# Compression products in quarters between the projection's column units, with bias tables, sigmoid and masks moved up

## The chip, the core and the metric

The kernel runs on one core of one Trainium2 chip. A core has TensorE (PE in the profile; its weight loads are PEld), VectorE (DVE), ScalarE (ACT), GpSimd (POOL) and SyncE (SP), and 16 DMA engines. TensorE runs at one of two clock levels, 1.2 or 2.4 GHz; the profile gives the granted clock as a share of the upper one (PEclk 1.00 or 0.50). The metric is the device time of one execution in microseconds (us); less is better.

## The reference, cut to what matters

The program is two transformer blocks in float32 over 512 positions of width 1024. Only the beginning of the first block is touched: the projection of the normalized input by `w_in`, the compression of two of its column groups (`kc`, `vc`), and the entry of the attention that follows.

```python
def nsa_compress(kraw, pos, w1, b1, w2):
    ch = kraw.reshape(b, g, s // CMP_STRIDE, CMP_STRIDE, dh)
    blk = jnp.concatenate([ch[:, :, :-1], ch[:, :, 1:]], axis=3) + pos
    hid = jax.nn.gelu(jnp.einsum('bgnld,ldh->bgnh', blk, w1) + b1)
    return hid @ w2
...
    xn = rms_norm(h, norm1_g[layer])
    aq, ak, av, bq, kc, vc, ksl, vsl, kw, vw, gl = split_columns(xn @ w_in[layer])
    o_a = mixer_dilated(to_heads(aq, A_HEADS), to_heads(ak, A_HEADS), to_heads(av, A_HEADS), tab_a)
    ...
    k_cmp = nsa_compress(to_heads(kc, B_KV_HEADS), cmp_pos[layer], cmp_k_w1[layer], ...)
    v_cmp = nsa_compress(to_heads(vc, B_KV_HEADS), cmp_pos[layer], cmp_v_w1[layer], ...)
```

`gl` passes through a sigmoid and gates three attention branches. Each head's scores get a bias by distance, which lies as a table per head in DRAM (`bias_spread`).

## The kernel before, in words

The program is a list of stages. Each engine goes through the stages in the same order, and at the end of each all four compute engines meet (`meet`: drain, count up, wait for the four; seen as L2712). SP alone runs ahead: it fills a ring of six weight slots of 1 MB (`Ring.fill`, L254), and for load n it waits until n - 5 slots have been given back (`weights_used`). A DMA from POOL or SP is only issued there; it lands later on a semaphore.

The stage in question is `Together(ModStart, BiasSpread, Load, InProjection)`. On POOL, `BiasSpread` writes the bias tables to DRAM (L933) and `Load` fetches small tensors (L752); nothing else is on POOL there. `InProjection` has six blocks of columns (0 to 5); each has two ring slots, and its work is cut into 28 units (0 to 27), each with a PSUM bank of its own out of banks 0 to 3. Blocks 2 to 5 have four units each of 16 recorded passes of 512 columns (L1040, or L1042 where rows of the input are the weights): units 12 to 15, 16 to 19, 20 to 23, 24 to 27. Even units are copied out of PSUM by DVE, odd ones by ACT (L324, L326, L327). At the end of a block PE drains and gives two slots back (L1046).

`Compress` sits whole behind block 3. DVE has built its inputs after block 2 (`blocks`, L986 and L987; tile `Z`). PE then runs 128 matmuls of 31 columns for K and V (L966, 256 recorded passes, four ring slots loaded by SP as `in_cmp_k_w` and `in_cmp_v_w`, each slot in two DMAs of 512 KB), each half followed by a drain (L969); ACT applies the gelu (L1002), and PE makes four small matmuls more (L973, L977), which DVE copies out (L993, L995).

Behind all units ACT takes the sigmoid of the gates (L1067) and DVE negates `sink`, casts `glamask` and multiplies the gates (L1080 to L1084). Then the engines meet, and `PairAttention` begins. Its first instructions on POOL load the bias tables of the first two packs of heads (`Z<-bias_spread`, L729, four DMAs of 256 KB). PE makes scores (L540), DVE adds the bias and takes the row minimum (L668, waits for the table), ACT takes the exponential (L604), PE transposes (L558) and multiplies by the values (L575). One set of score banks is in use, so the scores of the next unit wait for L668 of this one.

Of the kernel before, what the change touches and what calls it, by code (L numbers as in the profile page):

```python
# [21 lines left out]
P = 128  # L22
# [409 lines left out]
class PairAttention(Stage):  # L432
# [203 lines left out]
    def vector(self, dve, ch):  # L636
# [4 lines left out]
        for i in range(N + 4):  # L641
# [73 lines left out]
            self._copies(dve, "dve", i - 1)  # L715

    def gpsimd(self, pool, ch):
        k = self.k
        if self.loads:
            pool.wait_ge(k.bias_spread, 16)  # L720
        todo = list(self.extra.items())
        for q, heads in enumerate(self.loads):
            if q >= 2:

                while todo and self.packs[todo[0][0]]["load"] < q - 2:
                    self._sum(pool, *todo.pop(0))
                pool.wait_ge(k.bias_used.sem, self.b_used + q - 1)
            for h, src in enumerate(heads):
                pool.dma_start(k.bias[:, q % 2, h, :], src).then_inc(k.bias_landed[q % 2].sem, 16)  # L729
        for pi, x in todo:  # L730
            self._sum(pool, pi, x)
# [204 lines left out]
class Compress(Stage):  # L936


    def __init__(self, k, A, kraw, vraw):
        super().__init__(k)  # L940
        self.raw = [kraw, vraw]
        self.slots = []
        for w1 in (A["cmp_k_w1"][0], A["cmp_v_w1"][0]):
            for l0 in (0, 16):
                src = w1[l0:l0 + 16].rearrange("l d h -> d l h")
                parts = [((lambda s, g=g: s[64 * g:64 * g + 64, :].rearrange("p (l h) -> p l h", l=16)), src) for g in range(2)]
                self.slots.append(k.rg.plan(parts))
        self.blk_ready = k.step_done.reserve(2)
        self.hid_full = k.psum_full.reserve(2)
        self.hid_done = k.gates_done.reserve(2)  # L950
        self.kc_full = k.psum_full.reserve(2)
        self.blk = [k.cmpblk(i) for i in range(2)]
        self.hid = k.cmphid

    def tensor(self, pe):
        k = self.k
        for i in range(2):
            pe.wait_ge(k.step_done.sem, self.blk_ready + i + 1)
            for half in range(2):
                n = self.slots[2 * i + half]  # L960
                k.rg.await_landed(pe, n)
                w = k.rg.slot(n).rearrange("p (l h) -> p l h", l=16)
                for l in range(16):
                    for g in range(2):
                        ll = 16 * half + l
                        last = pe.matmul(k.ps[:, 4 + 2 * i + g, 0:NCMP], w[64 * g:64 * g + 64, l, :],  # L966
                                         self.blk[i][64 * g:64 * g + 64, :, ll], start=(ll == 0), stop=(ll == 31))
                k.rg.released(last)
            pe.drain().then_inc(k.psum_full.sem, 1)  # L969
# [26 lines left out]

    def scalar(self, act, ch):
        k = self.k
        for i in range(2):
            act.wait_ge(k.psum_full.sem, self.hid_full + i + 1)  # L1000
            for g in range(2):
                act.activation(self.hid[:, i, g * NCMP:(g + 1) * NCMP], k.ps[:, 4 + 2 * i + g, 0:NCMP],  # L1002
                               ACT.Gelu_apprx_tanh, bias=k.b1[:, i:i + 1])
            act.drain().then_inc(k.gates_done.sem, 1)


class InProjection(Stage):


    READY, INSIDE = 2, 3  # L1010

    def __init__(self, k, w, blocks, load, compress):
        super().__init__(k)
        self.slots, self.units, self.load = [], [], load
        for b, items in enumerate(blocks):
            c0, cn = items[0][1], sum(x[2] for x in items)
            self.slots.append((cn, [plan_columns(k, w, k0, 4, c0, cn) for k0 in (0, 4)]))
            for kind, at, n, dst, scale in items:
                self.units += [(b, kind, at - c0, n, t, dst, scale) for t in (range(ST) if kind == "rows" else [0])]
            if b == self.INSIDE:  # L1020
                self.compress = compress()
        owners = ["act" if dst is None else x for x, (*_, dst, _) in zip(alternate(len(self.units)), self.units)]
        self.banks = Banks(k, owners, 0, 4, lane=1)
        self.gated = k.step_done.reserve(1)

    def last_of(self, b):
        return max(u for u, x in enumerate(self.units) if x[0] == b)

    def tensor(self, pe):
        k = self.k  # L1030
        for u, (b, kind, at, n, t, _, _) in enumerate(self.units):
# [5 lines left out]
            for c in range(DK):  # L1037
# [3 lines left out]
                else:  # L1041
                    last = pe.matmul(self.banks.bank(u)[:, 0:n], k.HT[:, c, t * P:(t + 1) * P], w,  # L1042
                                     start=(c == 0), stop=(c == DK - 1))
            self.banks.filled(last)
            if u == self.last_of(b):
                pe.drain().then_inc(k.weights_used, 2)  # L1046
                if b == self.INSIDE:
                    self.compress.tensor(pe)

# [11 lines left out]
    def scalar(self, act, ch):  # L1061
        k = self.k
        for u, x in enumerate(self.units):
            self._take(act, "act", u)
            if u == self.last_of(self.INSIDE):
                self.compress.scalar(act, ch)
        act.activation(k.gate3[:, :, :], k.Zb(IN_W)[:, :, GL:GL + 24], ACT.Sigmoid).then_inc(k.step_done.sem, 1)  # L1067

    def vector(self, dve, ch):
        k = self.k  # L1070
        for u, x in enumerate(self.units):
            self._take(dve, "dve", u)
            if u == self.last_of(self.READY):
# [3 lines left out]
                self.compress.blocks(dve)  # L1077
            if u == self.last_of(self.INSIDE):
                self.compress.taken(dve)
        dve.tensor_scalar(k.sink[:, :], k.sink[:, :], -1.0, None, ALU.mult)  # L1080
        dve.tensor_copy(k.glamask[:, :, :], k.maskf)
        dve.wait_ge(k.step_done.sem, self.gated + 1)
        g = k.gate3[:, :, :].rearrange("p t (h b) -> p t h b", b=3)[:, :, :, 0]
        dve.tensor_tensor(g, g, k.cmpvalid[:, :].unsqueeze(2).to_broadcast((P, ST, 8)), ALU.mult)  # L1084

# [1239 lines left out]
def two_blocks(nc, A, C, out, scratch):  # L2325
    ctx = ExitStack()
    with ctx:
# [223 lines left out]
        def rows(at, n, mine=False):  # L2551
# [7 lines left out]
        start, spread, small = ModStart(k), BiasSpread(k, bias_rows, scratch["bias"], scratch["spread"]), Load(k, pairs)  # L2559
        add(Together(k, start, spread, small,  # L2560
                     InProjection(k, A["w_in"][0], blocks, small, lambda: Compress(k, A, rawT[:, 0, :], rawT[:, 1, :]))))

# [16 lines left out]
        for rr in range(4):  # L2579
# [9 lines left out]
            loads.append([bias_of(A_HEADS + rr), bias_of(A_HEADS + 4 + rr)])  # L2589
        add(PairAttention(k, packs, 512, 7168, 9216, 1, 4, loads))  # L2590

# [232 lines left out]
```

## Time and profile before

| | before |
|---|---|
| median of 3 runs | 2438.12 us (2437.29 to 2439.75) |
| the profiled execution | 2439.43 us, span 2437.6 us |
| mean granted clock | 0.925 |
| PE busy | 2093.0 us (86%) |
| DVE, ACT, POOL busy | 1001.9, 601.7, 183.2 us |

The page first gives busy time by engine, then the span in 40 slices (61 us each): the busy tenths of each engine, the clock granted to PE, and the share of the DMA engines. PE is busy 86% of the span, more than twice as long as any other engine, so a stretch of the program is read by when PE works, at which clock, and for what it waits. The page's own chain of waits covers only the last microseconds and says nothing on this stage; the timeline and the tables by stretch do.

### The profile page before, as it was taken

How to read it: one execution, taken by the hardware profiler on the slowest of the kernel's cores; microseconds unless marked ns; L12 is line 12 of the kernel's file. 1: busy time of each engine (PE TensorE's matmuls, PEld its weight loads, DVE VectorE, ACT ScalarE, POOL GpSimd, SP SyncE). 2: the span in 40 equal slices, each digit the busy share in tenths (PEclk: the TensorE clock that was granted, in tenths of full speed). 3: DMA queues.
4: the chain of work that ended last, by engine and by line, in shares of the span. 5: the costliest groups of instructions: out<-in, count | busy, mean ns of one | idle time of the engine just before them, and what ended most of it. 6: DMA issues, size and time to landing. Idle time of an engine off the chain costs nothing. (4 is left out here: it accounts for less than half of the span.)

```text
span 2437.6 us, 26968 instructions
## 1 busy us (share of the span) xinstructions
PE 2093.0 (86%) x10260; PEld 1126.0 (46%) x10260; DVE 1001.9 (41%) x1847; ACT 601.7 (25%) x1138; POOL 183.2 (8%) x219
## 2 busy tenths in 40 slices
PE   5998999899999996989988975999629688958993
PEld 3564774444444443565566453333225466443331
DVE  1001660478773003686344135223155655243333
ACT  1002660100000003322254022333231344023441
POOL 3000110011110000121000000000010000001001
PEclk9988999899999998999999976999859899968997
DMA  7532101476664212111010034777531000055994
GB/s 224 114 104 95 36 10 52 157 257 242 232 235 138 78 54 91 35 35 70 4 49 2 17 123 169 261 299 290 185 127 70 1 1 1 1 201 215 348 343 147
DMA packets 103757, 311.66 MB, mean 128 GB/s; under 512 B 8727, under 2 KB 42679, under 8 KB 85200
## 3 DMA queue, kind: packets, MB, share of 16 engines
q1 hardware_dynamic: 73360, 178.50, 21.1%
q0 software_dynamic: 23040, 105.19, 12.4%
q10 hardware_dynamic: 7232, 26.25, 2.8%
q8 instruction: 85, 1.39, 0.2%
q14 instruction: 40, 0.33, 0.0%
HBM read 280.47 MB, written 34.68 MB: 129 GB/s over the span
## 5 line engine op out<-in xcount | busy, mean ns | idle before, releaser
L2294 PE MATMUL ps<-wide 128*128 128x512 f32 x704 | 306.0, 594 | 2.1 <-issue 1.3
L2057 PE MATMUL ps<-wide,Z 128*64 x576 | 258.7, 603 | 3.5 <-DVE Z L2151 3.5
L2058 PE MATMUL ps<-T,Z 128*64 128x512 f32 x576 | 258.7, 602 | 0.0
L2294 PEld LDWEIGHTS ps<-wide 128*128 128x128 f32 x704 | 132.4, 190 | 171.6 <-issue 170.6
L294 PE MATMUL ps<-wide 128*128 128x512 f32 x448 | 196.8, 601 | 5.5 <-ACTq L2712 4.3
L604 ACT ACTIVATE T<-T,nm 128x128 f32<-128x128 f32 (+5 forms) x208 | 139.7, 672 | 176.3 <-DVE nm L668 176.3
L376 PE MATMUL ps<-ident,T 128*128 128x128 f32 x240 | 39.5, 345 | 143.5 <-DVE T L365 143.5
L558 PE MATMUL ps<-ident,T 128*128 128x128 f32 x752 | 116.1, 286 | 45.7 <-DVE T L326 26.9
L294 PE MATMUL ps<-wide,T 128*128 128x512 f32 x352 | 151.6, 593 | 0.9 <-ACTq L2712 0.7
L1358 PE MATMUL ps<-wide 128*128 128x512 f32 (+1 forms) x384 | 150.0, 548 | 0.5 <-issue 0.5
L2057 PEld LDWEIGHTS ps<-wide,Z 128*64 128x64 f32 x576 | 76.9, 138 | 156.7 <-issue 156.7
L294 PEld LDWEIGHTS ps<-wide 128*128 128x128 f32 x448 | 85.7, 192 | 114.8 <-issue 108.9
L540 PE MATMUL ps<-T 64*128 64x256 f32 (+1 forms) x960 | 120.8, 378 | 19.7 <-DVE nm L668 15.5
L2039 PE MATMUL ps<-wide,Z 128*64 x288 | 131.2, 598 | 4.4 <-ACT Z L2112 4.4
L860 DVE SCALAR_TENSOR_TENSOR Z<-Z,wide 128x2048 f32<-128x2048 f32 x56 | 131.6, 2350 | 3.2 <-DVE Z L860 0.5
L2040 PE MATMUL ps<-Z 128*64 128x512 f32 x288 | 131.3, 598 | 0.0
L558 PEld LDWEIGHTS ps<-ident,T 128*128 128x128 f32 x752 | 80.5, 142 | 78.6 <-ACT T L604 58.0
L1040 PE MATMUL ps<-wide 128*128 128x512 f32 x256 | 112.8, 601 | 1.9 <-issue 1.1
L575 PE MATMUL ps<-T,Z 128*64 128x128 f32 x1504 | 113.6, 295 | 0.3 <-DVE T L326 0.3
L324 ACT ACTIVATE T<-ps 128x256 f32<-128x256 f32 (+4 forms) x171 | 75.7, 455 | 141.5 <-PE ps L1040 103.3
L540 PEld LDWEIGHTS ps<-T 64*128 64x128 f32 x960 | 84.6, 200 | 48.1 <-DVE nm L668 21.8
L376 PEld LDWEIGHTS ps<-ident,T 128*128 128x128 f32 x240 | 38.3, 185 | 147.5 <-issue 147.5
(338 smaller groups left out, 2716.1 us busy)
## 6 DMA issues: line engine op xcount, KB each, us to landing
wide<-in_experts SPq DMA_DIRECT2D x96, 1024.0 KB, 6.2
Z<-in_mod_w POOLq DMA_DIRECT2D x32, 1024.0 KB, 5.2
moe_out<-Z ACTq DMA_DIRECT2D x36, 512.0 KB, 3.8
X<-in_mod_w POOLq DMA_DIRECT2D x16, 1024.0 KB, 5.2
wide<-in_w_gate SPq DMA_DIRECT2D x22, 512.0 KB, 5.1
wide<-in_w_up SPq DMA_DIRECT2D x22, 512.0 KB, 6.3
wide<-in_w_in SPq DMA_DIRECT2D x10, 1024.0 KB, 7.4
wide<-in_w_down SPq DMA_DIRECT2D x10, 1024.0 KB, 5.1
```

The costliest lines, as they stand in the source:

```text
L294: last = pe.matmul(self.banks.bank(u0 + i)[0:self.rows, 0:cn], self.lhs(k0 + c, t), w[:, c, :], start=(k0 + c == 0), stop=(k0 + c == self. ...
L540: last = pe.matmul(s, u["q"](h), kT(h)[:, done:done + m], start=True, stop=True)
L558: last = pe.transpose(self.t.bank(c)[:, b * P:(b + 1) * P], src, k.ident[:, :])
L575: last = pe.matmul(k.ps[64 * h:64 * h + 64, 7, ui * P:(ui + 1) * P], v(h), self.PT[:, j % 2, h, b * P:(b + 1) * P], start=(b == 0), stop=( ...
L604: act.activation(p, p, ACT.Exp, scale=-1.0, bias=k.nm[:, pi % 2, c:c + 1], accum_out=k.den[:, pi % 2, c:c + 1]).then_inc(k.probs_done.sem, 1)
L860: ins = dve.scalar_tensor_tensor(acc, w, by, acc, ALU.mult, ALU.add)
L1358: last = pe.matmul(self.lin.bank(u)[:, 0:cn], k.HT[:, c, t * P:(t + 1) * P], w[:, c % 4, :], start=(c == 0), stop=(c == DK - 1))
L2039: pe.matmul(ps[low, 5 + hf, :], mo.hidT[:, p, c, low], w.columns(e, 2, at), start=(c == 0), stop=(c == 1))
L2040: last = pe.matmul(ps[high, 5 + hf, :], mo.hidT[:, p, c, high], mo.wd[:, p, at:at + 512], start=(c == 0), stop=(c == 1))
L2057: pe.matmul(ps[low, p, :], mo.xT[:, p, c, low], w.columns(e, j, at), start=(c == 0), stop=(c == DK - 1))
L2058: last = pe.matmul(ps[high, p, :], mo.xT[:, p, c, high], mo.wgu[:, p, j, at:at + 512], start=(c == 0), stop=(c == DK - 1))
L2294: last = pe.matmul(self.gu.bank(u)[:, 0:self.n], w, self.rhs(c), start=(c == 0), stop=(c == DK - 1))
```

## The change

- `Compress` is no longer one piece. Its products go in quarters of 32 matmuls: the two of K behind units 16 and 18 (block 3), the two of V behind units 20 and 22 (block 4). The drain of each half remains. The four small matmuls come behind unit 24, and DVE's two copies after it behind its copy of unit 24.
- The ring's order follows: K's two slots between those of blocks 3 and 4, V's two between those of blocks 4 and 5. Blocks 3 and 4 give back four slots at their end; a quarter gives back none by itself.
- ACT's sigmoid comes behind its copy of unit 17, DVE's `sink`, `glamask` and gate product behind its copy of unit 18. The gelus stay behind units 19 and 23.
- POOL issues the four bias DMAs of the first two packs in the projection's stage, behind the small loads (`prefetch`); the attention's own loop begins with the third pack.

```diff
+    def prefetch(self, pool):
+        pool.wait_ge(self.k.bias_spread, 16)
+        for q in range(2):
+            self._load(pool, q)
...
+    def _load(self, pool, q):
+        for h, src in enumerate(self.loads[q]):
+            pool.dma_start(self.k.bias[:, q % 2, h, :], src).then_inc(self.k.bias_landed[q % 2].sem, 16)
...
-    READY, INSIDE = 2, 3
+    READY, INSIDE, END = 2, (3, 4), 5
...
             self.banks.filled(last)
+            i = u - self.last_of(b) + 3
+            if b in self.INSIDE and i % 2 == 0:
+                self.compress.products(pe, self.INSIDE.index(b), i // 2)
+            if b == self.END and i == 0:
+                self.compress.tensor(pe)
             if u == self.last_of(b):
-                pe.drain().then_inc(k.weights_used, 2)
-                if b == self.INSIDE:
-                    self.compress.tensor(pe)
+                pe.drain().then_inc(k.weights_used, 4 if b in self.INSIDE else 2)
...
-            if u == self.last_of(self.INSIDE):
-                self.compress.scalar(act, ch)
-        act.activation(k.gate3[:, :, :], k.Zb(IN_W)[:, :, GL:GL + 24], ACT.Sigmoid).then_inc(k.step_done.sem, 1)
+            if u == self.last_of(self.READY) + 2:
+                act.wait_ge(k.step_done.sem, self.compress.blk_ready + 2)
+                act.activation(k.gate3[:, :, :], k.Zb(IN_W)[:, :, GL:GL + 24], ACT.Sigmoid).then_inc(k.step_done.sem, 1)
+            if x[0] in self.INSIDE and u == self.last_of(x[0]):
+                self.compress.gelu(act, self.INSIDE.index(x[0]))
```

The instructions of PE from block 1 to the attention's first scores, before the change (names are those of the words above; 32 matmuls of 512 columns are one block):

```order
L1042 MATMUL ps<-wide 128x152 x32
L1040 MATMUL ps<-wide 128x512 x64
L966 MATMUL ps<-Z,wide 128x31 x128
L973 MATMUL ps<-Z,w 64x31 x2
L977 MATMUL ps<-w,Z 31x64 x2
L1042 MATMUL ps<-wide 128x512 x32
L1040 MATMUL ps<-wide 128x512 x32
L540 MATMUL ps<-T 128x128 x2
```

The same stretch after it, up to the middle of block 5:

```order
L1050 MATMUL ps<-wide 128x512 x40
L971 MATMUL ps<-Z,wide 128x31 x32
L1050 MATMUL ps<-wide 128x512 x16
L971 MATMUL ps<-Z,wide 128x31 x32
L1050 MATMUL ps<-wide 128x512 x8
L1052 MATMUL ps<-wide 128x512 x8
L971 MATMUL ps<-Z,wide 128x31 x32
L1052 MATMUL ps<-wide 128x512 x16
L971 MATMUL ps<-Z,wide 128x31 x32
L1052 MATMUL ps<-wide 128x512 x8
L1050 MATMUL ps<-wide 128x512 x8
L980 MATMUL ps<-Z,w 64x31 x2
```

The one run of 128 small matmuls has become four of 32, with 16 large ones between neighbours.

SP's ring loads from the compression's first slot on, before the change:

```order
L254 DMA wide<-in_cmp_k_w 64x16x128 [waits weights_used]
L254 DMA wide<-in_cmp_k_w 64x16x128
L254 DMA wide<-in_cmp_k_w 64x16x128 [waits weights_used]
L254 DMA wide<-in_cmp_k_w 64x16x128
L254 DMA wide<-in_cmp_v_w 64x16x128 [waits weights_used]
L254 DMA wide<-in_cmp_v_w 64x16x128
L254 DMA wide<-in_cmp_v_w 64x16x128 [waits weights_used]
L254 DMA wide<-in_cmp_v_w 64x16x128
L254 DMA wide<-in_w_in 128x4x512 [waits weights_used] x4
```

And after it:

```order
L254 DMA wide<-in_cmp_k_w 64x16x128 [waits weights_used]
L254 DMA wide<-in_cmp_k_w 64x16x128
L254 DMA wide<-in_cmp_k_w 64x16x128 [waits weights_used]
L254 DMA wide<-in_cmp_k_w 64x16x128
L254 DMA wide<-in_w_in 128x4x512 [waits weights_used] x2
L254 DMA wide<-in_cmp_v_w 64x16x128 [waits weights_used]
L254 DMA wide<-in_cmp_v_w 64x16x128
L254 DMA wide<-in_cmp_v_w 64x16x128 [waits weights_used]
L254 DMA wide<-in_cmp_v_w 64x16x128
L254 DMA wide<-in_w_in 128x4x512 [waits weights_used] x2
```

V's slots have moved behind block 4's: they are loads 12 and 13 of the ring now and were 10 and 11, so they wait for slots 7 and 8 to be given back (end of block 3) and no longer for 5 and 6 (end of block 2).

ACT from its copies of blocks 2 and 3 to the attention's first exponential, before the change:

```order
L324 ACTIVATE T<-ps 128x512 [waits psum_full_1] x4
L1002 ACT_TABLE_LOAD
L1002 ACTIVATE Z<-ps,b 128x31 [waits psum_full_0]
L1002 ACTIVATE Z<-ps,b 128x31
L1002 ACTIVATE Z<-ps,b 128x31 [waits psum_full_0]
L1002 ACTIVATE Z<-ps,b 128x31
L324 ACTIVATE Z<-ps 128x512 [waits psum_full_1] x2
L324 ACTIVATE T<-ps 128x512 [waits psum_full_1] x2
L1067 ACT_TABLE_LOAD
L1067 ACTIVATE gate<-Z 128x96
L604 ACT_TABLE_LOAD [waits scores_topped]
```

And after it:

```order
L324 ACTIVATE T<-ps 128x512 [waits psum_full_1] x3
L1080 ACT_TABLE_LOAD
L1080 ACTIVATE gate<-Z 128x96 [waits step_done]
L324 ACTIVATE T<-ps 128x512 [waits psum_full_1]
L1008 ACT_TABLE_LOAD
L1008 ACTIVATE Z<-ps,b 128x31 [waits psum_full_0]
L1008 ACTIVATE Z<-ps,b 128x31
L324 ACTIVATE Z<-ps 128x512 [waits psum_full_1] x2
L1008 ACTIVATE Z<-ps,b 128x31 [waits psum_full_0]
L1008 ACTIVATE Z<-ps,b 128x31
L324 ACTIVATE T<-ps 128x512 [waits psum_full_1] x2
L604 ACT_TABLE_LOAD [waits scores_topped]
```

The number of table loads is the same; the sigmoid's one stands between copies now, and the last thing in the stage is the copy of unit 27.

## Rows read from the trace of the kernel before

**Rows 1.** Page, parts 1 and 2: PE's busy time; its tenths and clock by slice.

```profile
PE 2093.0 (86%) x10260; PEld 1126.0 (46%) x10260; DVE 1001.9 (41%) x1847; ACT 601.7 (25%) x1138; POOL 183.2 (8%) x219
...
PE   5998999899999996989988975999629688958993
...
PEclk9988999899999998999999976999859899968997
```

**Rows 2.** Timeline of PE: start us, us, line, tile, count, idle before it.

```profile
108.97 27.70 PE L1040 MATMUL ps<-wide 128*128 128x512 f32 x64 [0.29 <-issue]
136.93 9.06 PE L966 MATMUL ps<-Z,wide 64*128 64x31 f32 x128 [0.26 <-issue]
146.25 13.87 PE L966 MATMUL ps<-Z,wide 64*128 64x31 f32 x128 [0.26 <-issue]
160.74 0.43 PE L973 MATMUL ps<-Z,w 128*64 128x31 f32 x4 [0.62 <-ACTq L1004]
161.10 0.64 PE L977 MATMUL ps<-w,Z 128*31 128x64 f32 x4
161.67 29.94 PE L1042 MATMUL ps<-wide 128*128 128x512 f32 x64
191.87 27.70 PE L1040 MATMUL ps<-wide 128*128 128x512 f32 x64 [0.26 <-issue]
222.12 0.49 PE L540 MATMUL ps<-T 64*128 64x128 f32 x4 [2.55 <-DVEq L2712]
230.03 1.23 PE L540 MATMUL ps<-T 64*128 64x256 f32 x4 [7.42 <-DVE nm L668]
231.68 0.86 PE L558 MATMUL ps<-ident,T 128*128 128x128 f32 x2 [0.43 <-ACT T L604]
```

**Rows 3.** Table by stretch around L966: length, busy (count), then PEclk, DMA share, GB/s.

```profile
core 0: us, PE busy (x) PEld busy (x) DVE busy (x) ACT busy (x) POOL busy (x), PEclk, DMA share, GB/s
139.00:140.00 1.00, 1.00 (x23) 1.00 (x21) 0.00 (x0) 0.00 (x0) 0.00 (x0) 1.00 1.04 389
142.00:143.00 1.00, 1.00 (x17) 1.00 (x15) 0.00 (x0) 0.00 (x0) 0.00 (x0) 0.62 1.03 393
148.00:149.00 1.00, 1.00 (x12) 1.00 (x13) 0.00 (x0) 0.00 (x0) 0.00 (x0) 0.50 0.99 362
165.00:166.00 1.00, 1.00 (x2) 0.33 (x1) 0.00 (x0) 0.00 (x0) 0.00 (x0) 0.50 0.00 0
167.00:168.00 1.00, 1.00 (x4) 0.52 (x3) 0.00 (x0) 0.00 (x0) 0.00 (x0) 1.00 0.00 0
```

**Rows 4.** The same table in a later stage, around a short fall of the clock.

```profile
1080.00:1081.00 1.00, 1.00 (x12) 0.80 (x9) 1.00 (x3) 1.00 (x1) 0.00 (x0) 0.95 0.00 0
1084.00:1085.00 1.00, 1.00 (x5) 0.90 (x4) 1.00 (x1) 0.00 (x0) 0.61 (x1) 0.84 0.00 0
```

**Rows 5.** Landing times in us of `in_cmp_v_w`, windows 108.7:109 and 108.7:109.5; then table by stretch.

```profile
wide<-in_cmp_v_w SPq DMA_DIRECT2D x1, 512.0 KB, 5.3
...
wide<-in_cmp_v_w SPq DMA_DIRECT2D x2, 512.0 KB, 6.2
...
119.00:120.00 1.00, 1.00 (x4) 0.48 (x3) 0.00 (x0) 0.00 (x0) 0.00 (x0) 1.00 0.97 170
```

**Rows 6.** Timeline of ACT at the end of the stage and the attention's entry.

```profile
219.61 0.60 ACT L324 ACTIVATE T<-ps 128x512 f32<-128x512 f32 x1 [13.14 <-PE ps L1040]
220.22 1.28 ACT L1067 ACT_TABLE_LOAD   x1
221.52 0.28 ACT L1067 ACTIVATE gate<-Z 128x96 f32<-128x96 f32 x1
229.84 1.28 ACT L604 ACT_TABLE_LOAD   x1 [8.04 <-DVE nm L668]
```

**Rows 7.** Timelines of DVE and POOL there.

```profile
221.83 0.20 DVE L1084 TENSOR_TENSOR gate<-gate,cmpvalid 128x32 f32<-128x32 f32 x1 [7.79 <-ACT gate L1067]
229.46 0.29 DVE L668 CUSTOM_DVE_ANT_0 T<-ps,Z 128x128 f32<-128x128 f32 x1 [7.43 <-DMA Z<-bias_spread]
...
222.36 2.13 POOL L729 DMA_DIRECT2D Z<-bias_spread  x4 [167.88 <-DVEq L2712]
```

**Rows 8.** Table by stretch: after block 1's first unit, and at the attention's entry.

```profile
72.00:80.00 8.00, 8.00 (x62) 7.76 (x61) 0.00 (x0) 1.49 (x4) 0.00 (x0) 1.00 0.05 17
...
237.00:238.00 1.00, 1.00 (x6) 0.35 (x5) 0.15 (x1) 0.00 (x0) 0.00 (x0) 0.59 0.00 0
```

More of the change, by code:

```diff
@@ L715, in vector @@
             self._copies(dve, "dve", i - 1)
+    def prefetch(self, pool):
[5 more added lines that the diff above has]
+            pool.dma_start(self.k.bias[:, q % 2, h, :], src).then_inc(self.k.bias_landed[q % 2].sem, 16)
     def gpsimd(self, pool, ch):
         k = self.k
-        if self.loads:
-            pool.wait_ge(k.bias_spread, 16)
         todo = list(self.extra.items())
[L722 to L729, printed above, removed]
+        for q in range(2, len(self.loads)):
+            while todo and self.packs[todo[0][0]]["load"] < q - 2:
+                self._sum(pool, *todo.pop(0))
+            pool.wait_ge(k.bias_used.sem, self.b_used + q - 1)
+            self._load(pool, q)
         for pi, x in todo:
@@ L940, in __init__ @@
         super().__init__(k)
[L941 to L947, printed above, removed]
+        self.raw, self.slots, self.w1 = [kraw, vraw], [], [A["cmp_k_w1"][0], A["cmp_v_w1"][0]]
         self.blk_ready = k.step_done.reserve(2)
@@ L953, in __init__, with plan, products @@
         self.hid = k.cmphid
+    def plan(self, i):
+        for l0 in (0, 16):
+            src = self.w1[i][l0:l0 + 16].rearrange("l d h -> d l h")
+            parts = [((lambda s, g=g: s[64 * g:64 * g + 64, :].rearrange("p (l h) -> p l h", l=16)), src) for g in range(2)]
+            self.slots.append(self.k.rg.plan(parts))
+    def products(self, pe, i, half):
+        k = self.k
+        if half == 0:
+            pe.wait_ge(k.step_done.sem, self.blk_ready + i + 1)
+        n = self.slots[2 * i + half]
+        k.rg.await_landed(pe, n)
+        w = k.rg.slot(n).rearrange("p (l h) -> p l h", l=16)
+        for l in range(16):
+            for g in range(2):
+                ll = 16 * half + l
+                last = pe.matmul(k.ps[:, 4 + 2 * i + g, 0:NCMP], w[64 * g:64 * g + 64, l, :],
+                                 self.blk[i][64 * g:64 * g + 64, :, ll], start=(ll == 0), stop=(ll == 31))
+        if half:
+            pe.drain().then_inc(k.psum_full.sem, 1)
     def tensor(self, pe):
         k = self.k
[L957 to L969, printed above, removed]
         pe.wait_ge(k.gates_done.sem, self.hid_done + 2)
@@ L995, in taken, with gelu @@
         dve.tensor_copy(k.vcmp[0:NCMP, :], k.ps[0:NCMP, 5, 0:2 * HD])
-    def scalar(self, act, ch):
+    def gelu(self, act, i):
         k = self.k
[L999 to L1004, printed above, removed]
+        act.wait_ge(k.psum_full.sem, self.hid_full + i + 1)
+        for g in range(2):
+            act.activation(self.hid[:, i, g * NCMP:(g + 1) * NCMP], k.ps[:, 4 + 2 * i + g, 0:NCMP],
+                           ACT.Gelu_apprx_tanh, bias=k.b1[:, i:i + 1])
+        act.drain().then_inc(k.gates_done.sem, 1)
 class InProjection(Stage):
-    READY, INSIDE = 2, 3
+    READY, INSIDE, END = 2, (3, 4), 5
     def __init__(self, k, w, blocks, load, compress):
         super().__init__(k)
-        self.slots, self.units, self.load = [], [], load
+        self.slots, self.units, self.load, self.compress = [], [], load, compress
         for b, items in enumerate(blocks):
@@ L1024, in __init__, with gpsimd @@
         self.gated = k.step_done.reserve(1)
+        self.early = None
+    def gpsimd(self, pool, ch):
+        self.early.prefetch(pool)
     def last_of(self, b):
@@ L2559, in two_blocks @@
         start, spread, small = ModStart(k), BiasSpread(k, bias_rows, scratch["bias"], scratch["spread"]), Load(k, pairs)
-        add(Together(k, start, spread, small,
-                     InProjection(k, A["w_in"][0], blocks, small, lambda: Compress(k, A, rawT[:, 0, :], rawT[:, 1, :]))))
+        projection = InProjection(k, A["w_in"][0], blocks, small, Compress(k, A, rawT[:, 0, :], rawT[:, 1, :]))
+        add(Together(k, start, spread, small, projection))
         def bias_of(h):
@@ L2589, in two_blocks @@
             loads.append([bias_of(A_HEADS + rr), bias_of(A_HEADS + 4 + rr)])
-        add(PairAttention(k, packs, 512, 7168, 9216, 1, 4, loads))
+        projection.early = PairAttention(k, packs, 512, 7168, 9216, 1, 4, loads)
+        add(projection.early)
         def mixT_units(w, starts, tiles):
```

17 lines of the change are left out of this document (9 added, 8 removed).

## The prediction, made before the changed kernel was run

> **What bounds the kernel now.** I read the page first: PE is busy 86% of the span and granted nearly full clock in most slices [rows 1]. The change touches one stretch of some 100 us near the start, so I went to PE's timeline there, for idle time and for the same work at different speeds [rows 2], then to the table by stretch for the granted clock [rows 3], then to the other engines where PE waits [rows 6, 7], and last to SP's DMAs, whose order changes [rows 5].
>
> PE is the path from block 3 to block 5. Its only waits are drains of 0.26 us and the gelu's 0.62. But it is not always at full speed. L966's first 128 passes take 9.06 us and the second 128 take 13.87, and block 4 takes 29.94 where blocks 3 and 5 take 27.70 [rows 2]. The clock explains all three: 23 passes per us at PEclk 1.00, 12 or 13 at 0.50, with the fall at about 142.6, and 2 passes per us in block 4 until about 166, then 4 [rows 3]. So the small matmuls run at 2.4 GHz for 5.7 us, then at 1.2 GHz until 4.4 us of block 4 have passed.
>
> At the entry of the attention PE is idle 2.55 us, works 0.49 and is idle 7.42 more [rows 2]. The first gap is ACT's sigmoid and DVE's gate product before the engines meet [rows 6, 7]. The second is L668, which waits for the bias table; POOL issues it at 222.36 only, and it has landed at 229.46 [rows 7]. In that idle time the clock falls again and comes back at 237.6 [rows 8].
>
> **The change part by part.** Each term is in us of this one profiled execution.
>
> *T1, the small matmuls.* The 256 passes take 22.93 in all. At 23 per us [rows 3] they take 11.13: -11.8, if the clock holds.
>
> *T2, gaps and second layer.* Three gaps (0.26, 0.26, 0.62) become three drains of 0.26: -0.4. Behind unit 24 the gelu of V has had a whole unit (27.70 / 4 = 6.9) against its 0.5 us of work, so nothing waits. L973 and L977 take 0.93 at 1.2 GHz; at 2.4 about half: -0.4. Together -0.8.
>
> *T3, block 4 at full clock:* 29.94 to 27.70, -2.2.
>
> *T4, V's first slot.* This is the wait that the change adds. The slot's two DMAs were issued from 108.75 and had 28 us and more to land. Now they are issued at the end of block 3, and PE needs the slot one drain and one unit later, 0.26 + 6.92 = 7.2. The first DMA lands after 5.3, the mean of the first two is 6.2, so the second lands after 7.1 from its own issue [rows 5], and it is issued some 0.5 after the first: 7.7 after the block's end. +0.5, bounded by 0 and 1.5 (an issue later by 1 us). Queued behind this wait on PE are V's quarter and all of block 4; DVE and ACT have nothing else to do. K's slots, issued at block 1's end as before, and block 4's own, issued at block 2's end, land within 12 us (the four DMAs from 108.75 are done soon after 120 [rows 5]) and have 28 or more.
>
> *T5, the clock in the quarters.* A quarter is 64 passes, 2.8 us; the run before it fell had 5.7 us of them. Between two quarters lie 13.8 us of large matmuls. The trace has no such pattern, so I bound it: 0 if the clock holds, and if it falls, the shortest stay at the lower level seen, 3.4 us between 1081 and 1085 [rows 4], costs half of itself, 1.7. Four falls cost 6.8. A quarter with its drain is half as long as what was survived at full clock, but it stands close to it; I take one fall, +1.7.
>
> A rule of the Trainium skill can be held against this term. PE's busy share is 1.00 on both sides of the fall at 142.6 [rows 3]. The page TensorE: Matmul & The Clock Gate, section What's actually happening, says that the gate follows how busy the PE has been recently. With busy as the profile counts it, the clock would hold in the quarters, T5 would be 0 and the sum -24.9; but by the same reading it would not have fallen at 142.6. The trace disagrees with that reading, so I go by the rows.
>
> *T6, the tail.* Without table load, sigmoid and gate product, ACT's copy ends at 220.21 [rows 6] and DVE has long been done. PE starts 0.1 after the last engine now (DVE ends at 222.03, PE starts at 222.12), so at 220.3: -1.8. The moved work costs nothing: the sigmoid's 1.56 us on ACT and about 1 us on DVE stand behind copies 17 and 18, whose engines otherwise wait 13 us for their next unit [rows 6]. If that cover were gone, each would delay a bank by its own length.
>
> *T7, the bias.* POOL is free and the DMA share is 0.05 from 72 to 80 [rows 8], so the 1 MB that takes 7.1 us at 222 lands some 130 us early. L668 then follows the scores, at 222.61 instead of 229.46: -6.8. Late next is ACT's table load of 1.28, which stands behind L668 in both kernels.
>
> *T8, the entry's clock.* Before, PE worked from 231.68 to 237.6 at 1.2 GHz without idling; at 2.4 that is half of 5.9, -2.9. But PE is sparse for 3 to 4 us at the new entry too, so the clock may fall there once for 3.4 us: -1.2. I take -2.0.
>
> Nothing else moves: no instruction is added on PE, and the later stages begin behind a meeting of all engines, so they shift as a whole.
>
> The sum: -11.8 - 0.8 - 2.2 + 0.5 + 1.7 - 1.8 - 6.8 - 2.0 = **-23.2**. From the profiled execution's 2439.4 that gives 2416.2; that execution is 1.3 above the median, so from 2438.1 the forecast is **2414.9 us**.
>
> **The rivals.**
>
> *A, the clock falls at each quarter and stays down as long as after the single run.* Block 4 needed 4.4 us to bring it back; four times 4.4 at half speed costs 8.8 instead of 1.7. The sum is -16.1, 2422.0. For it: the fall came in work of the same kind. Against: 5.7 us of it went by first.
>
> *B, V's first slot lands with all that is issued then.* V's 2 MB and block 5's 2 MB are issued together; V's took until 120.9 after 108.75 and 2 MB more take about 5, so the last lands 17 us after the block's end and PE would wait 10 instead of 0.5: -13.7, 2424.4. Against: the first DMA landed after 5.3 with three behind it, so they land in order.
>
> *C, the prefetch brings nothing,* because something else of the same length stands before L668. Then T7 and T8 go: -14.4, 2423.7. Nothing in the rows has that length.
>
> *D, slower: the clock does not come back between the quarters.* The three units left of block 3, block 4 and unit 24 (20.8 + 27.7 + 6.9 = 55.4) then take twice as long, and the quarters 11.1 more: -24.9 + 66.5 = +41.6, 2480. It decides from the point where the stays at 1.2 GHz cost more than the 24.9 of the other terms, that is 12.5 us after each quarter of the 13.8 that follow. Block 4 brought the clock back in 4.4 [rows 3].
>
> **How the numbers follow.** Forecast 0.76, A 0.12, B 0.06, C 0.04, D 0.02. The forecast's own bounds: T4 0, T5 0, T8 -2.9 give -26.3, 2411.8; T4 1.5, T5 6.8, T8 -1.2 give -16.3, 2421.8. A lies at the upper one; B, C and D (0.12) stay outside. The runs before spread by 0.8 below and 1.6 above their median. Range 2411.0 to 2422.5. About 0.2% (5 us) is what a measurement of this kernel can tell from no change; only D and mishaps unnamed lie on the other side: faster 0.97, within 0.01, slower 0.02.
>
> **What would show it.** After: the quarters at 23 passes per us and 2.8 us each; block 4's passes at 27.7 us without the quarters; a gap of about 0.5 before V's first quarter; PE's first scores 0.75 after the end of block 5; L668 right behind them with no wait for a DMA. PEclk at 0.50 between the quarters speaks for A, or D if it lasts. A gap of 10 us before V's first quarter is B. The forecast is wrong if the gain up to the attention's first scores is not near 15 us, or if the attention's first pack takes back what its entry gave.

## The result and the profile after

The changed kernel takes **2423.5 us** (median of 13 runs, 2410.4 to 2429.1) against 2438.2 (13 runs of before beside them, 2433.8 to 2442.9). The ratio is 0.9931, 95% interval 0.9919 to 0.9943: a gain of 0.7%, some 16.8 us by the ratio and 14.7 by the medians. The forecast was 23.2. The sign holds and the ratio's time, 0.9931 x 2438.1 = 2421.3, lies inside the range, but about a third of the expected gain is missing. Of all runs in this document one, of 2698.4 us at a granted clock of 0.81, was in a slower state of the chip, and it is left out of its kernel's median.

The profiled execution of after took 2424.7 us, its span 2422.9 (before: 2439.4 and 2437.6), so the two traces differ by the same 14.7. Its timeline of PE, from the start of block 3 to the attention's first scores (columns as in [rows 2], whose lines these answer; L971 is what L966 was, L1050 and L1052 the units of odd and even blocks):

```profile
108.17 7.10 PE L1050 MATMUL ps<-wide 128*128 128x512 f32 x16 [0.26 <-issue]
115.20 3.77 PE L971 MATMUL ps<-Z,wide 64*128 64x31 f32 x64
118.90 14.00 PE L1050 MATMUL ps<-wide 128*128 128x512 f32 x32
132.83 3.77 PE L971 MATMUL ps<-Z,wide 64*128 64x31 f32 x64
136.69 8.82 PE L1050 MATMUL ps<-wide 128*128 128x512 f32 x16
145.77 7.11 PE L1052 MATMUL ps<-wide 128*128 128x512 f32 x16 [0.26 <-issue]
154.20 3.91 PE L971 MATMUL ps<-Z,wide 64*128 64x31 f32 x64 [1.32 <-DMA wide<-in_cmp_v_w]
158.04 15.50 PE L1052 MATMUL ps<-wide 128*128 128x512 f32 x32
173.47 3.77 PE L971 MATMUL ps<-Z,wide 64*128 64x31 f32 x64
177.32 8.82 PE L1052 MATMUL ps<-wide 128*128 128x512 f32 x16
...
193.44 0.31 PE L980 MATMUL ps<-Z,w 128*64 128x31 f32 x4
193.68 0.41 PE L984 MATMUL ps<-w,Z 128*31 128x64 f32 x4
194.02 20.87 PE L1050 MATMUL ps<-wide 128*128 128x512 f32 x48
215.61 0.49 PE L540 MATMUL ps<-T 64*128 64x128 f32 x4 [0.72 <-ACTq L2729]
216.86 0.70 PE L540 MATMUL ps<-T 64*128 64x256 f32 x4 [0.76 <-DVE nm L668]
```

The reader sees three things. The quarters take 3.77 us each, not 2.8. A unit of 16 passes takes 7.1 us in most places and 8.82 at 136.7 and 177.3; the pair at 158.0 takes 15.50 where the one at 118.9 takes 14.00. And PE waits 1.32 us for V's first slot. The table by stretch shows that the slow units are the clock, and that PE was never idle there (columns as in [rows 3]):

```profile
116.20:117.20 1.00, 1.00 (x22) 1.00 (x20) 0.00 (x0) 0.00 (x0) 0.00 (x0) 1.00 0.08 16
137.00:138.00 1.00, 1.00 (x2) 0.34 (x1) 0.00 (x0) 0.00 (x0) 0.00 (x0) 0.60 0.00 0
158.00:159.00 1.00, 1.00 (x3) 0.50 (x2) 0.00 (x0) 0.00 (x0) 0.00 (x0) 0.50 1.00 319
178.00:179.00 1.00, 1.00 (x3) 0.38 (x2) 0.00 (x0) 0.00 (x0) 0.00 (x0) 0.58 0.00 0
219.00:220.00 1.00, 1.00 (x5) 0.79 (x7) 0.17 (x1) 0.99 (x5) 0.00 (x0) 0.56 1.06 356
```

The clock goes to its lower level three times in the stretch, behind K's second quarter and both of V's, for 3.4 us each (8.82 - 7.1 = 1.7 is half of it), and once at the entry of the attention.

The entry went as meant. The bias DMAs are issued at 71.7, L668 runs 0.69 us after the first scores instead of 7.34, and the table load follows it (timelines of POOL, DVE and ACT, against [rows 6, 7]):

```profile
71.69 2.13 POOL L725 DMA_DIRECT2D Z<-bias_spread  x4 [16.27 <-DMA rb<-in_router_expert_b]
...
216.30 0.29 DVE L668 CUSTOM_DVE_ANT_0 T<-ps,Z 128x128 f32<-128x128 f32 x1 [7.55 <-PE ps L540]
...
214.93 0.60 ACT L324 ACTIVATE T<-ps 128x512 f32<-128x512 f32 x1 [13.14 <-PE ps L1050]
216.67 1.28 ACT L604 ACT_TABLE_LOAD   x1 [1.15 <-DVE nm L668]
```

**Where the time went.** From the start of block 3 to the end of block 5 the two traces take 110.60 and 106.72 us: -3.9, where the forecast has -12.6. From there to the end of the attention's first L585, -9.5, forecast -10.6. Ahead of block 3, -0.8, which the change doesn't touch. That is -14.2 at the end of that first pack (244.5 and 230.3), against a forecast of -23.2. Behind it nothing moves that belongs to the change, but two later stages show how far the clock's own chance goes (table by stretch; the first two lines are one stage of before and of after, the last is the end of after's span, 354.0 us where before took 350.7 from 2086.9 to 2437.6):

```profile
371.84:447.47 75.63, 64.99 (x161) 31.63 (x161) 11.62 (x18) 8.50 (x14) 0.00 (x0) 0.87 0.18 56
...
357.29:429.39 72.10, 61.46 (x161) 29.94 (x161) 11.62 (x18) 8.50 (x14) 0.00 (x0) 0.93 0.19 58
...
2068.90:2422.90 354.00, 280.74 (x1204) 123.73 (x1204) 111.71 (x239) 96.42 (x126) 27.07 (x29) 0.87 0.58 216
```

The same 161 passes take 3.5 us less in after, where less of the stage ran at the lower level (granted clock 0.93 instead of 0.87), and the last stretch gives 3.3 back. These cancel in this pair of traces. What is left to explain is mainly the compression; 1.1 us is missing at the entry.

### The profile page after: what moved, and what is told of

The parts are those of the page before. It is cut to its first block and busy times, and to the rows that moved or that the text cites. A ratio compares the mean times of both kernels' runs of the same rounds, so it can differ in the third digit from the quotient of the medians.

```text
span 2422.9 us, 26969 instructions
## 1 busy us (share of the span) xinstructions
PE 2088.5 (86%) x10260; PEld 1118.9 (46%) x10260; DVE 1001.1 (41%) x1847; ACT 601.6 (25%) x1138; POOL 183.5 (8%) x219
## 5 line engine op out<-in xcount | busy, mean ns | idle before, releaser
L376 PE MATMUL ps<-ident,T 128*128 128x128 f32 x240 | 40.8, 352 | 143.5 <-DVE T L365 143.5
L558 PE MATMUL ps<-ident,T 128*128 128x128 f32 x752 | 121.7, 296 | 41.9 <-DVE T L326 22.5
L540 PE MATMUL ps<-T 64*128 64x256 f32 (+1 forms) x960 | 116.5, 368 | 11.7 <-DVE nm L668 9.3
L558 PEld LDWEIGHTS ps<-ident,T 128*128 128x128 f32 x752 | 84.4, 147 | 75.7 <-ACT T L604 55.6
L1050 PE MATMUL ps<-wide 128*128 128x512 f32 x256 | 113.6, 602 | 2.0 <-issue 1.1
L376 PEld LDWEIGHTS ps<-ident,T 128*128 128x128 f32 x240 | 39.6, 189 | 147.5 <-issue 147.5
L294 PEld LDWEIGHTS ps<-wide,T 128*128 128x128 f32 x352 | 66.7, 190 | 85.1 <-issue 84.2
## 6 DMA issues: line engine op xcount, KB each, us to landing
wide<-in_w_in SPq DMA_DIRECT2D x10, 1024.0 KB, 10.2
```

Source lines behind the costliest of these rows:

```text
L294: last = pe.matmul(self.banks.bank(u0 + i)[0:self.rows, 0:cn], self.lhs(k0 + c, t), w[:, c, :], start=(k0 + c == 0), stop=(k0 + c == self. ...
L540: last = pe.matmul(s, u["q"](h), kT(h)[:, done:done + m], start=True, stop=True)
L558: last = pe.transpose(self.t.bank(c)[:, b * P:(b + 1) * P], src, k.ident[:, :])
```

## The experiments

The theory behind the first ones: the entry gives what was forecast, and the compression is short of its forecast because the quarters take longer than reckoned and because the clock falls beside them. Open is what makes it fall: the length of a run of small matmuls, or the drain or the wait that stands next to it. "The stretch" is from the start of block 3 to the end of block 5, 110.60 us before and 106.72 after. All kernels compute the whole reference. A time without an interval is that of a single run.

### The two halves of the change, each alone

The compression in one piece behind block 3, as before, but with the bias loaded early and sigmoid and masks moved up:

```
-            if b in self.INSIDE and i % 2 == 0:
-                self.compress.products(pe, self.INSIDE.index(b), i // 2)
...
+                if b == 3:
+                    for q in range(4):
+                        self.compress.products(pe, q // 2, q % 2)
+                    self.compress.tensor(pe)
```

> The compression stays in one piece behind block 3 as before; only the prefetch of the bias tables and the earlier sigmoid and masks are kept. Theory: the entry's gain does not need the quarters. PE's gap after block 5 is 0.7 us instead of 2.55, L668 follows the first scores by about 0.7 instead of 7.3 us, the first pack ends about 1 us shorter: 1.8 + 6.9 + 1.0 = 9.7 us faster than before, 2428.5. Rival (the entry's gain is smaller alone because the clock falls there whatever lands): under 8 us.

Measured: 2427.0 us, ratio 0.9949 (0.9932 to 0.9967). The stretch is 110.58, as before; first pack's end at 234.7, 9.8 before that of before.

The other half, quarters alone, with bias, sigmoid and masks where they were:

```
-    def gpsimd(self, pool, ch):
-        self.early.prefetch(pool)
...
-            if u == self.last_of(self.READY) + 2:
-                act.wait_ge(k.step_done.sem, self.compress.blk_ready + 2)
-                act.activation(k.gate3[:, :, :], k.Zb(IN_W)[:, :, GL:GL + 24], ACT.Sigmoid).then_inc(k.step_done.sem, 1)
```

> The quarters and the ring's new order are kept; the bias tables are issued in the attention, sigmoid and masks stand at the stage's end as before. Theory: 256 passes cost 15.1 us (4 x 3.77) instead of 22.93, gaps and second layer 0.9 less, block 4's slow start 2.2 less, the wait for V's first slot 1.3 more: 9.6 us faster than before, less 1.7 for each fall of the clock after a quarter. With one to three falls 4.5 to 8 us faster, 2430 to 2434. Rival (the forecast's own size, quarters of 2.8 us): 12 us faster, 2426.

Measured: 2434.3 us, 0.9974 (0.9963 to 0.9985). The stretch is 106.47, with three falls of 3.4 us and a wait of 1.06, and both idle gaps at the entry are back (timeline of PE, this kernel):

```profile
216.58 0.49 PE L540 MATMUL ps<-T 64*128 64x128 f32 x4 [2.55 <-DVEq L2727]
224.49 1.23 PE L540 MATMUL ps<-T 64*128 64x256 f32 x4 [7.41 <-DVE nm L668]
```

The median lies at the slow edge of the expected 2430 to 2434, and the rival's 2426 fell. The halves give 0.51% and 0.26%, together 0.77% against 0.69% for the whole. So the entry is two thirds of the gain and near its forecast (-9.5 us in the traces, forecast -10.6); most of the shortfall is in the quarters.

### Eighths

Eight steps behind every unit instead of sixteen behind every second one. `products` takes the steps l0 to l1 - 1:

```
-            if b in self.INSIDE and i % 2 == 0:
-                self.compress.products(pe, self.INSIDE.index(b), i // 2)
+            if b in self.INSIDE:
+                at = ((0, 8, 16, 24, 32), (0, 8, 16, 24, 32))[self.INSIDE.index(b)]
+                self.compress.products(pe, self.INSIDE.index(b), at[i], at[i + 1])
```

> The changed kernel, but with the products in eighths of 16 matmuls behind each unit of blocks 3 and 4; drains and the wait for V's first slot stay. Theory (a sparse run of 3.8 us lets the clock fall, one of 1.9 us does not): no PEclk of 0.50 from block 3 to block 5, the stretch from block 3's start to block 5's end is 5.1 us shorter than the changed kernel's 106.7, the median about 3 to 5 us under 2423. Rival (drain or wait beside the sparse run makes it fall; the one quarter without either, K's first, kept its clock): the same falls behind V's first piece and behind the two drained ones, within 1 us of the changed kernel.

Measured: 2422.0 us, 0.9928 (0.9909 to 0.9948). The stretch is 103.44, with one fall, at V's first piece, which is also the one that waits for its DMA (timeline of PE, then the table by stretch up to that piece's end and behind it):

```profile
116.61 7.13 PE L1052 MATMUL ps<-wide 128*128 128x512 f32 x16
...
151.68 1.98 PE L973 MATMUL ps<-Z,wide 64*128 64x31 f32 x32 [0.61 <-DMA wide<-in_cmp_v_w]
153.59 8.82 PE L1054 MATMUL ps<-wide 128*128 128x512 f32 x16
...
107.67:153.50 45.83, 44.86 (x240) 24.06 (x240) 2.80 (x6) 4.88 (x8) 0.00 (x0) 1.00 0.34 86
153.50:157.20 3.70, 3.70 (x9) 1.66 (x8) 0.00 (x0) 0.00 (x0) 0.00 (x0) 0.54 1.11 272
```

Seven of eight pieces held the clock. That one beside the wait did not leaves the drain or the wait as a rival, which the next kernel tries. The median did not follow the trace: 3 to 5 us under 2423 were expected, and the ratio of 0.9928 can't be told from the changed kernel's 0.9931.

### Quarters with V's moved one unit later

```
+                at = ((0, 16, 16, 32, 32), (0, 0, 16, 16, 32))[self.INSIDE.index(b)]
```

> The changed kernel, but with V's two quarters behind units 21 and 23 instead of 20 and 22, so that V's first slot has 14 us to land instead of 7. Theory (it lands 8.5 us after block 3's end): PE's wait of 1.3 us before V's first quarter is gone, the falls of the clock stay as they are: about 1.3 us faster than the changed kernel, 2422. Rival (the wait also set off the fall behind V's first quarter): 3 us faster, and no PEclk of 0.50 behind it.

Measured: 2423.0 us, 0.9928 (0.9907 to 0.9948), again not to be told from the changed kernel. No wait is left. The stretch is 103.44, with two falls, behind K's first quarter and V's first, neither of which has a drain or a wait beside it (table by stretch):

```profile
119.00:123.00 4.00, 4.00 (x7) 1.70 (x6) 0.00 (x0) 0.00 (x0) 0.00 (x0) 0.57 0.00 0
...
163.50:167.50 4.00, 4.00 (x7) 1.70 (x6) 0.00 (x0) 0.00 (x0) 0.00 (x0) 0.57 0.00 0
```

So a quarter amid large matmuls, with PE busy throughout, is enough for a fall. The rival that a drain or a wait is needed goes; that a wait makes a fall likelier is another matter, and comes up again below.

### Eighths for K, three pieces a unit later for V

```
+                at = ((0, 8, 16, 24, 32), (0, 0, 11, 22, 32))[self.INSIDE.index(b)]
```

> The changed kernel with K's products in eighths behind each unit of block 3, and V's in three pieces of 11, 11 and 10 steps (22, 22 and 20 matmuls) behind units 21, 22 and 23. Theory (a piece of up to 2.6 us with large matmuls on both sides keeps the clock, and V's first slot has landed by then): no fall from block 3 to block 5, no wait; the stretch from block 3's start to block 5's end is 101 us (103.4 with eighths, less the wait of 0.6 and the fall of 1.7), 5.7 less than the changed kernel's 106.7; median near 2418 to 2420. Rival (sparse pieces let the clock fall by chance however short they are): falls remain and the stretch stays at 103.

Measured: 2415.4 us (2414.5 to 2418.3), 0.9902 (0.9885 to 0.9918). The stretch is 102.45: no wait, and one fall of 3.4 us where none was expected, behind V's first piece of 22 matmuls (44 passes). Run again under another name, with the changed kernel beside it on the same chip:

> The kernel of e5 once more, beside the changed kernel on one chip. Theory: 102.5 us or less for the stretch, K's eighths without a fall again, at most one fall among V's three pieces, and 5 to 8 us faster than the changed kernel's median. Rival (e5's 2415.4 was luck of the later stages): within 3 us of it.

> The changed kernel itself, timed on the same chip as e9 and e10. Theory: 2421 to 2426, ratio to the kernel before 0.993, one to four falls among its quarters and a wait of 0.8 to 1.4 us before V's first. Rival (the quarters' falls come seldom, e8's single one is the rule): under 2420 with none or one.

Measured: 2419.9 us, 0.9914 (0.9901 to 0.9926), against 2423.4, 0.9931 (0.9916 to 0.9945), for the changed kernel. The 3.5 us between the medians lie between theory's 5 to 8 and the rival's 3; the trace of the changed kernel has one fall, of 6.8 us. In this form the stretch had no fall at all this time and took 100.76 us (table by stretch, then the timeline of PE where the first trace had its fall):

```profile
108.78:209.50 100.72, 100.00 (x456) 50.99 (x456) 5.16 (x11) 7.14 (x13) 0.00 (x0) 1.00 0.35 105
...
158.99 2.65 PE L973 MATMUL ps<-Z,wide 64*128 64x31 f32 x44
161.57 7.13 PE L1054 MATMUL ps<-wide 128*128 128x512 f32 x16
```

The first comparison puts this form ahead of the changed kernel by 0.3%, the second by 0.17% with intervals that overlap. It is the fastest form run here, by a little.

### Without the prefetch

The whole change, but the bias loaded where it was before (`prefetch` and its call gone, the two loads back behind the engines' meeting).

> The changed kernel, but POOL issues the first four bias DMAs in the attention again; quarters, sigmoid and masks stay. Theory (the entry's wait was the landing of the tables, whatever stands before it): L668 waits for the DMA again, 7 to 7.4 us behind the first scores, the clock then stays down for over 10 us; 6.9 + 1.0 = about 8 us slower than the changed kernel, 2431.5. Rival (the DMAs in the attention land faster when ACT's tail is gone): under 5 us slower.

Measured: 2429.5 us, 0.9962 (0.9948 to 0.9976), 0.31% or some 7.5 us more than with it. L668 waits for the DMA again (DVE, then PE):

```profile
221.06 0.29 DVE L668 CUSTOM_DVE_ANT_0 T<-ps,Z 128x128 f32<-128x128 f32 x1 [14.24 <-DMA Z<-bias_spread]
...
221.62 1.22 PE L540 MATMUL ps<-T 64*128 64x256 f32 x4 [7.46 <-DVE nm L668]
```

### Halves

```
+                at = ((0, 32, 32, 32, 32), (0, 0, 32, 32, 32))[self.INSIDE.index(b)]
```

> The changed kernel with K's products in one piece of 64 matmuls behind unit 16 and V's in one piece behind unit 21. Theory (the longer the sparse run, the surer and the longer the clock is down): both pieces of 7.4 us fall to 0.50 in or behind them, 3.4 to 6.8 us each; the stretch from block 3's start to block 5's end is 104 to 107 us against 100 without any fall. Rival (only the number of pieces counts): two falls of 3.4 us, 103.4.

Measured: 2424.2 us, a single run; the stretch is 107.71. The two halves, of 128 passes each, take 8.69 and 9.87 us, and the stays at the lower level are mostly longer than those beside a quarter: 6.8 and 10.2 us. Both the second stay and the stretch are longer than theory and rival had them (timeline, then table by stretch):

```profile
117.61 8.69 PE L973 MATMUL ps<-Z,wide 64*128 64x31 f32 x128
...
163.27 9.87 PE L973 MATMUL ps<-Z,wide 64*128 64x31 f32 x128
...
126.39:131.00 4.61, 4.61 (x7) 2.07 (x8) 0.00 (x0) 0.00 (x0) 0.00 (x0) 0.59 0.00 0
163.27:173.10 9.83, 9.83 (x129) 9.74 (x128) 0.00 (x0) 0.60 (x1) 0.00 (x0) 0.73 0.36 133
```

### The changed kernel once more

> The changed kernel once more. Theory (which quarter lets the clock fall is chance, since K's first quarter kept it in one run and lost it in another kernel's): two to four falls among the four quarters, not all at the same places as before; the stretch from block 3's start to block 5's end between 105 and 108.4 us. Rival (the places are fixed by the program): falls behind K's second and both of V's quarters again, 106.7.

Measured: 2427.9 us, a single run. The same program now has one fall in the stretch, of 6.8 us, at V's first quarter, where theory had two at least; before that quarter the clock is 1.00 throughout, behind K's second too, where the first trace had its first fall (table by stretch, then the timeline of PE at V's first quarter; the last two lines are the same places in the third trace of the changed kernel, the one timed beside the last form):

```profile
110.84:157.00 46.16, 44.91 (x249) 24.42 (x250) 2.80 (x6) 4.89 (x8) 0.00 (x0) 1.00 0.35 87
157.00:165.00 8.00, 8.00 (x36) 4.60 (x35) 0.00 (x0) 0.00 (x0) 0.00 (x0) 0.57 0.95 291
...
154.75 4.34 PE L971 MATMUL ps<-Z,wide 64*128 64x31 f32 x64 [0.90 <-DMA wide<-in_cmp_v_w]
...
155.00:162.00 7.00, 7.00 (x27) 3.89 (x25) 0.00 (x0) 0.00 (x0) 0.00 (x0) 0.51 0.98 313
...
152.35 4.49 PE L971 MATMUL ps<-Z,wide 64*128 64x31 f32 x64 [0.96 <-DMA wide<-in_cmp_v_w]
```

Which quarters lose the clock differs from one execution to the next. This is not the chip alone: the kernel without the prefetch ran on the same chip as this one, with the same stretch, and its trace has falls at K's first quarter and at both of V's. So one trace can't tell which quarter is the bad one.

The wait before V's first piece is not cleared, though. All six pieces of 16 matmuls or more that stood behind a wait for their DMA lost the clock (five quarters and one eighth), and of the 40 quarters and shorter pieces without such a wait only 9 did. A wait is not needed, as the kernel with V later shows, but whether it makes a fall likelier no run here tells: the wait and the place of V's first piece come together in all six.

### One step behind every large matmul

If short pieces are safe, are the shortest best? One step (4 small passes) behind each large matmul of K's four units and one or two behind each of V's three:

```
...
+                if b in self.INSIDE:
+                    j = self.INSIDE.index(b)
+                    p = (u - self.last_of(b) + 3 - j) * DK + c
+                    if p >= 0:
+                        n_at = (4 - j) * DK
+                        self.compress.products(pe, j, p * 32 // n_at, (p + 1) * 32 // n_at)
```

> The changed kernel with the products spread as finely as they go: one step of two small matmuls behind every large matmul of block 3 (K), one or two steps behind every large matmul of units 21 to 23 (V). Theory (the clock falls only where small matmuls stand together; a piece costs 0.1 us beyond its passes, as the eighths showed): no fall and no wait from block 3 to block 5, but 56 pieces cost up to 5.6 us: a stretch of 100 to 106 us, 2416 to 2421. Rival (the small matmuls cost nothing between large ones because their weight loads hide): 97 to 100 us and faster than every other form, 2412 to 2414.

Measured: 2434.6 us (eight runs), 0.9978 (0.9963 to 0.9993). The clock never fell, and the stretch takes 116.5 us, longer than before the change (table by stretch, then the pattern in the timeline of PE):

```profile
107.58:224.00 116.42, 115.70 (x456) 50.75 (x456) 5.16 (x11) 7.14 (x13) 0.00 (x0) 1.00 0.30 91
...
108.60 0.42 PE L973 MATMUL ps<-Z,wide 64*128 64x31 f32 x4
108.95 1.12 PE L1052 MATMUL ps<-wide 128*128 128x512 f32 x2
110.01 0.42 PE L973 MATMUL ps<-Z,wide 64*128 64x31 f32 x4
```

The first eleven periods in the trace take 1.40 us each. Their parts in long runs are 27.70 / 32 = 0.87 for a large matmul of two passes and 4 x 0.055 = 0.22 for the small ones: 0.31 us is lost at each piece, and 56 pieces lose 17. Theory had expected 106 us at most and the rival 100; going back and forth between the two shapes has a price that was 0.1 us in the theory and nothing in the rival.

## Why the forecast was a third too large

Take the stretches of all these traces together. "Stay" is the time at the lower clock level in the stretch.

| kernel | pieces | wait | stays | stretch | 100.3 + wait + half the stays |
|---|---|---|---|---|---|
| after | 4 | 1.32 | 3 x 3.4 | 106.72 | 106.7 |
| quarters only | 4 | 1.06 | 3 x 3.4 | 106.47 | 106.5 |
| no prefetch | 4 | 0.78 | 3 x 3.4 | 106.18 | 106.2 |
| changed, again | 4 | 0.90 | 6.8 | 104.59 | 104.6 |
| changed, timed | 4 | 0.96 | 6.8 | 104.65 | 104.7 |
| V later | 4 | none | 2 x 3.4 | 103.44 | 103.7 |
| eighths | 8 | 0.61 | 3.4 | 103.44 | 102.6 |
| eighths, V later | 7 | none | 3.4 | 102.45 | 102.0 |
| the same, again | 7 | none | none | 100.76 | 100.3 |
| halves | 2 | none | 6.8 + 10.2 | 107.71 | 108.8 |

The last column, fitted by its constant on the four-piece rows alone, holds for these within 0.3 us. Each piece more adds some 0.15 to 0.2, and the two-piece row lies 1.1 below.

**T1, the small matmuls: mis-sized, and the largest error.** The forecast divided 256 passes by "23 per us" and got 11.13 us. The count in a table by stretch is of matmuls that touch the window. Each lasts 0.278 us (mean, by shape, of after's first quarter) and starts 0.055 after the one before (3.77 less 0.28, over 63), so a window of 1 us counts the 18 that start in it and the four or five that reach into it; after's own line 116.20:117.20 says x22 at that same rate.

```profile
L971 PE MATMUL ps<-Z,wide 64*128 64x31 f32 x64 | 3.8, 278 | 0.0
```

The right number stood in [rows 2]: 128 passes at the lower level take 13.87 us, 0.108 each, so 0.054 at full clock, 64 of them 3.5, and 0.3 more for the last one to end. Measured 3.77, 3.77, 3.91 and 3.77, together 15.2 instead of 22.93: -7.7, not -11.8. That is 4.1 of the 8.7 us that are missing in the stretch.

**T2, gaps and second layer: -0.8, measured about -1.0.** L980 and L984 start right behind the unit and take 0.58 from the first's start to the unit behind them, 0.35 less; the gap of 0.62 is gone, and behind the two drained quarters PE is idle for 0.09 only (132.83 + 3.77 to 136.69), not 0.26.

**T3, block 4's slow start: -2.2, right.** It ends with a fall of its own in after, but that is T5's.

**T4, the wait for V's first slot: 0.5, measured 1.32** (0.61 to 1.06 in the other kernels with it), inside its bounds. SP's issues begin at 145.59 and PE goes on at 154.20; the first two DMAs landed after 6.9 us in the median, not 6.2 (issues of after from 145 to 146.9):

```profile
wide<-in_cmp_v_w SPq DMA_DIRECT2D x2, 512.0 KB, 6.9
```

The first slot did not wait for what was issued behind it: block 5's first load, issued at 151.50, took 10.1 us and was still on its way at 154.20. So rival B (10 us) fell.

**T5, the falls beside the quarters: 1.7, measured 5.1.** The forecast took one fall of four. Over the six traces with quarters (24 of them) 13 had a fall beside them: V's first in all six, V's second in three, K's in two each. Each stay cost half of its length, as reckoned; the length was 3.4 us, and 6.8 in two traces. The step that failed was "I take one": the 5.7 us that the single run survived were read as room, though a quarter stood, as the text said, close to it. Among the pieces without a wait before them, 8 of 19 quarters fell and 1 of 21 of the pieces of 16 to 22 matmuls (32 to 44 passes). So in these runs pieces of 2.0 to 2.65 us mostly kept the clock, and pieces of 3.8 us did not. The counts come from nine traces, one execution each.

The sum for the stretch: -7.7 - 1.0 - 2.2 + 1.3 + 5.1 = -4.5, measured -3.9. The other 0.6 is put down to the borders of the pieces, for which the forecast had no term: a unit that stands alone takes 7.10 or 7.11, where a quarter of a block is 6.9, and two together 14.00, where half a block is 13.85.

**The rule that was weighed.** PE's busy share is 1.00 in all three windows where the clock reads 0.50 to 0.60 in after, and in both of the kernel with V later. The Trainium skill, TensorE: Matmul & The Clock Gate, section HAM oscillation — how this bites in real kernels, gives as its rule that there be no idle gaps of PE above a certain length. Here no such gap was there (from the start of block 3 to the fall behind K's second quarter the longest in after is 0.09 us) and the clock fell, so on these small matmuls the trace disagrees with that rule, as the forecast had it; and the term that it would have set to 0 was already forecast too low.

**T6, the tail: -1.8, measured -1.83** (idle 2.55 to 0.72). **T7, the bias: -6.8, measured -6.65** in the pair of traces and 0.31% in the kernel without the prefetch, so rival C fell. **T8, the entry's clock: -2.0, measured -1.06.** The stretch from L668 to the end of the first L585 takes 14.0 instead of 15.06 us, with one stay of 3.4 at 219; that is near the bound of -1.2. In the first trace of the eighths with V later the entry had no fall and the same stretch took 12.8 us (-2.3); in the changed kernel's second trace it had 6.8 us of it and took 15.3. It differs from execution to execution as well.

**The rivals.** A's number (2422.0) is near what came, with other parts: three falls and not four, 3.4 us and not 4.4, and the rest is T1. D fell: in every trace with the products in pieces the clock came back within 10.2 us.

**The chances.** The median of 13 is a little above the range's top, the ratio's time inside; the pair of traces, with 14.7 less, gives 2423.4, outside by a little. That the time by the ratio lies inside is partly luck: no bound of the range had room for T1's error of 4.1 us, and it was covered by room meant for more falls. The changed kernel's runs spread over 19 us and those of before beside them over 9, but 18 runs of before, beside the first four experiments, spread over 21 too. The three traces of the changed kernel show a part of it: the stretch takes 104.6 to 106.7 us, the entry 13.9 to 15.3 from L668 to the end of the first L585, and block 3 begins between 108.2 and 110.8. The rest lies in other stages and was not followed up. What stays open: which property of the small matmuls (64 of 128 rows, 31 columns, or both) lets the clock fall while PE is busy. No run here changed their shape. Nor is it shown why V's first quarter fell every time, in five traces of six behind a wait.

## What to carry to other kernels

A rate is to be taken from start to start over a whole group (its time over its count), never from the count of a short window, where long overlapping instructions are counted at both edges. Many small matmuls in a row lowered TensorE's clock here though it was never idle. Cut into pieces of 2.0 to 2.65 us amid large ones they mostly kept it, pieces of 3.8 us did so about half the time, and pieces of 0.4 us lost more at their borders than the clock was worth. By the ratios the shorter pieces brought 0.03%, 0.29% and 0.17% over the quarters in three comparisons. The surest part was a load issued early: 1 MB issued 150 us before took 6.7 us off, and the wait was gone in every trace with it.

## What the runs showed of the hardware

- The granted clock fell with PE's busy share at 1.00, during or within about 1 us behind runs of 64 x 31 f32 matmuls, mostly of 3.8 us and longer, once behind one of 2.65 and once behind one of 1.98 that had waited for its DMA. The stays that a quarter brings are 3.4 or 6.8 us, those of halves 6.8 and 10.2. In which pieces they come differs between executions of one program. All six pieces behind a wait for their DMA fell.
- These matmuls (passes) start every 0.055 us at the higher level and every 0.106 at the lower ((13.87 - 0.40) / 127), and are shown as lasting 0.28 and 0.40 each.
- Going from large to small f32 matmuls and back costs 0.2 to 0.3 us: 0.31 at each of 56 pieces, most of four passes, and 0.28 at an eighth (a unit and its eighth follow every 8.97 us, their parts are 6.92 and 32 x 0.055 = 1.77).
- The two loads that V's first piece needs, issued at the end of block 3 with the rest of V's and block 5's behind them, kept PE waiting for 0.6 to 1.3 us in all six traces that need them one unit later; one unit more and there was no wait.
